# Four edits around TensorE's gaps: a shorter way into the first weights, earlier turned tiles for two output projections, and wider feed-forward matmuls

## The chip, the cores and the metric

One core of one Trainium2 chip runs the whole network for one sequence. The time is that of one execution on the device, in microseconds; kernels are compared by the median of their runs.

The engines each have a queue of their own and meet only at semaphores: TensorE (PE) multiplies and transposes, PEld is its weight load, VectorE (DVE), ScalarE (ACT) and GpSimd (POOL) compute, SyncE (SP) starts most loads.

## The reference

256 tokens, 1024 channels, float32, four layers in a row.

```
x = x + [forgetting attention (16 heads) * silu(ga), dilated attention (16 heads) * silu(gb)] @ even_w_out
x = x + (group_norm(retention(q, k, v), 4 heads of 512) * silu(g)) @ odd_w_out
x = rms_norm(x) ; h = x + rms_norm([ssm mixer, window attention] @ w_out)
h = h + rms_norm((silu(hn @ w_gate) * (hn @ w_up)) @ w_down),  hn = rms_norm(h), D_FF = 2816
```

Before each layer's input projection stands an RMS norm with a gain per channel. `h` is the output. Retention decays with distance, and its result is normalised per token and head before the gate. A row factor of an RMS norm (one number per token) can be applied after a product, since it scales whole rows.

## The kernel before, in words

**Weights.** They are read once, in 232 units of 128 x 1024 numbers (512 KB). A table (`weight_chunks`) puts them in order, in chunks of 4 to 11 units: ga, gb, qa, ka, va, qb, kb, vb (two each), even_out, then rq, rk (two each), rv, rg (four each), odd_out, then the mixer's, then eleven ffn chunks, then down. Four buffers (`RING`) each hold the raw unit (`stage`), its high part (`w_hi`, in the format fp32r, made by ScalarE, line 585) and its low part (`w_lo`, raw less high, by VectorE, line 841). SyncE loads unit u once the low part of unit u - 4 is made. ScalarE splits unit u once TensorE has used unit u - 3. `ahead(name)` on either engine splits up to three units beyond a chunk. An engine's queue is in order, so where a split stands among the other work is part of the design.

**Products.** Activations too have a high and a low part (`act_t`: tiles 0 to 7 high, 8 to 15 low; `y_lo` for the low parts of 16-tile inputs). Every product is made in three passes, high x high, activations' high x weights' low, activations' low x weights' high. `tokens_unit` (line 1404) keeps activations stationary and streams 512 weight columns. `channels_unit` (1421) and `ffn_unit` (1436) keep weights stationary and stream the 256 tokens.

**Turning.** Activations must have channels on partitions. TensorE transposes 128 x 128 blocks against an identity into a PSUM bank, ScalarE copies them as high tiles, VectorE subtracts to get the low ones. `turn_x` with `turn_rows` (1350) does this for x; `turn_wide` (1375) for the 16-tile inputs of even_out and odd_out, all 32 transposes before the first matmul, with `hi_of_wide` (632) and `lo_of_wide` (883) behind.

**Beginning.** TensorE multiplies ones (`keep_busy`, 1458), waits for the identity and the 84 rows of gains and parameters, turns these (1464), multiplies ones again, then turns x. ScalarE splits unit 0, makes eight high tiles, splits unit 1; VectorE likewise with the low ones. POOL issues small loads, `wf` (forget gate weights, 16 columns of a wide matrix) third.

**Heads of the even layer.** `attend` runs the heads through scores, exponentials, transposes and values; each eight heads are gated into gate_a and gate_b by POOL (446) and VectorE (`gate_heads`, 1032; semaphore `heads_out`).

**Retention.** During chunks rv the four heads' scores and values are made, and VectorE centres them (`ret_center`). During chunks rg 0 to 3 ScalarE drains silu(g) into gate1 (724), and VectorE multiplies the normalised head in (`ret_gate`, 1130; `ret_out`): head 0 in chunk rg 1, and so on, head 3 after rg 3.

**Feed-forward.** A chunk is 256 gate and 256 value channels, four units. VectorE takes both from PSUM times the norm's factor of each token (`rstd_row`; 1319), ScalarE applies silu (815), POOL multiplies (562), ScalarE and VectorE split the product (810, 1307) for the down projection. Two chunks' results fit in four banks. `row_of_diag` (1358) makes the factor row after chunk 0.

## Time and profile before

| | us |
|---|---|
| median of 3 runs | 820.35 |
| lowest, highest | 814.86, 823.98 |
| the profiled execution | 818.44 |
| its span | 816.6 |
| TensorE busy | 784.9 (96%) |
| weight load of TensorE, busy | 700.4 (86%) |
| VectorE busy | 520.3 (64%) |
| ScalarE busy | 393.0 (48%) |
| GpSimd busy | 216.8 (27%) |

The busy time of matmuls overlaps, since they are pipelined: the time per matmul is read from the distance of their starts, or from a long piece of the chain divided by its count. An L number is a line of the kernel. The loads move 160 GB/s on average over the span.

### The profile page before, as it was taken

The page shows a single profiled execution, that of the slowest core. Times are in us where ns is not written, and L with a number is a line of the kernel's source. Part 1 is how long each engine was busy: PE and PEld are TensorE (multiplying, and loading weights), DVE is VectorE, ACT ScalarE, POOL GpSimd, SP SyncE. Part 2 cuts the span into 40 slices and gives each one's busy share as a digit, 9 for nine tenths or more (in the row PEclk, how much of TensorE's full clock was granted, in tenths as well). Part 3 has the DMA queues.
Part 4 walks back from the last instruction along what each step waited for, and adds up shares of the span by engine and source line. Part 5 has one row for each costly group of instructions (what it writes and reads, how often), then busy time and mean ns, then how long its engine had stood idle before and what let it go on. Part 6 is the DMA issues. An engine that isn't in the chain of part 4 may idle for free.

```text
span 816.6 us, 13338 instructions
## 1 busy us (share of the span) xinstructions
PE 784.9 (96%) x5469; PEld 700.4 (86%) x5469; DVE 520.3 (64%) x756; ACT 393.0 (48%) x617; POOL 216.8 (27%) x180
## 2 busy tenths in 40 slices
PE   7999999999998999999999899998998999999997
PEld 6789987899877889987778788887777999999885
DVE  4846785864567557866568845775668666666553
ACT  5654446434455454344334535716766443544451
POOL 3022893470811000036019800144002110111010
PEclk9999999999999999999999999999999999999999
DMA  7897892587611554654545455520263665555651
GB/s 212 195 252 208 218 233 75 123 193 170 156 49 54 181 179 155 208 169 143 155 128 180 155 181 181 179 81 2 92 219 124 190 202 181 181 176 185 205 182 51
DMA packets 77824, 130.75 MB, mean 160 GB/s; under 512 B 4415, under 2 KB 28211, under 8 KB 77635
## 3 DMA queue, kind: packets, MB, share of 16 engines
q1 hardware_dynamic: 76418, 125.00, 52.8%
q0 software_dynamic: 1200, 4.83, 2.1%
q8 instruction: 43, 0.70, 0.3%
q14 instruction: 19, 0.15, 0.1%
q10 hardware_dynamic: 144, 0.07, 0.0%
HBM read 128.82 MB, written 1.06 MB: 159 GB/s over the span
## 4 chain that ended last, share of the span: by engine, by line
PE 88%; DVE 7%; DMA 2%; issue 1%; ACT 1%; POOL 1%; SPq 0%; DVEq 0%; POOLq 0%; ACTq 0%
PE ps L1404 41%; PE ps L1421 17%; PE ps L1436 16%; PE ps L1500 2%; PE ps L1519 2%; DMA stage<-in_even_w_in 2%; PE ps L1530 1%; PE ps L1800 1%; PE ps L1532 1%; PE ps L1531 1%; PE ps L1680 1%; DVE w_lo L841 1%; DVE act_t L878 1%; PE ps L1768 1%; PE ps L1630 1%
## 5 line engine op out<-in xcount | busy, mean ns | idle before, releaser
L841 DVE TENSOR_TENSOR w_lo<-stage,w_hi 128x1024 fp32r<-128x1024 f32 x232 | 306.6, 1339 | 177.4 <-ACT w_hi L585 176.9
L585 ACT ACTIVATE w_hi<-stage 128x1024 fp32r<-128x1024 f32 x232 | 244.0, 1062 | 264.6 <-PE ps L1404 129.1
L1404 PE MATMUL ps<-w_hi,act_t 128*128 128x512 f32 (+1 forms) x752 | 246.3, 391 | 3.4 <-DVE act_t L878 2.3
L1404 PEld LDWEIGHTS ps<-w_hi,act_t 128*128 128x128 f32 x752 | 140.6, 188 | 34.6 <-issue 3.6
L1404 PE MATMUL ps<-w_lo,act_t 128*128 128x512 f32 (+1 forms) x440 | 170.1, 387 | 0.0
L1421 PE MATMUL ps<-act_t,w_hi 128*128 128x256 f32 x832 | 151.9, 283 | 0.0
L1421 PEld LDWEIGHTS ps<-act_t,w_hi 128*128 128x128 f32 x832 | 130.8, 193 | 0.2 <-DVE w_lo L841 0.2
L1436 PE MATMUL ps<-act_t,w_hi 128*128 128x256 f32 x704 | 127.2, 283 | 0.7 <-DVE act_t L878 0.7
L1421 PE MATMUL ps<-act_t,w_lo 128*128 128x256 f32 x416 | 117.6, 283 | 0.0
L1436 PEld LDWEIGHTS ps<-act_t,w_hi 128*128 128x128 f32 x704 | 109.9, 192 | 0.9 <-issue 0.9
L1436 PE MATMUL ps<-act_t,w_lo 128*128 128x256 f32 x352 | 99.6, 283 | 0.0
L1404 PEld LDWEIGHTS ps<-w_lo,act_t 128*128 128x128 f32 x440 | 83.1, 189 | 16.8 <-issue 1.0
L1421 PEld LDWEIGHTS ps<-act_t,w_lo 128*128 128x128 f32 x416 | 80.2, 193 | 0.1
L1436 PEld LDWEIGHTS ps<-act_t,w_lo 128*128 128x128 f32 x352 | 67.6, 192 | 0.0
L1404 PE MATMUL ps<-w_hi,y_lo 128*128 128x512 f32 x128 | 50.3, 393 | 0.0
L562 POOL TENSOR_TENSOR big<-big 128x512 f32<-128x512 f32 x11 | 14.3, 1298 | 109.0 <-ACT big L815 109.0
L675 ACT ACTIVATE prob<-prob,neg_max 128x256 f32<-128x256 f32 x40 | 20.2, 505 | 22.5 <-DVE neg_max L1015 22.1
L1404 PE MATMUL ps<-w_hi,ff_hi 128*128 128x512 f32 x76 | 29.6, 389 | 0.0
L1404 PE MATMUL ps<-w_lo,ff_hi 128*128 128x512 f32 x76 | 29.6, 389 | 0.0
L1404 PE MATMUL ps<-w_hi,ff_lo 128*128 128x512 f32 x76 | 29.6, 389 | 0.0
L1404 PEld LDWEIGHTS ps<-w_hi,y_lo 128*128 128x128 f32 x128 | 24.3, 190 | 5.2
L405 POOL TENSOR_TENSOR sumsq<-sumsq,sumsq_b 128x2 f32<-128x2 f32 x2 | 0.4, 196 | 97.6 <-ACT junk L601 97.6
(347 smaller groups left out, 1029.9 us busy)
## 6 DMA issues: line engine op xcount, KB each, us to landing
stage<-in_even_w_in SPq DMA_DIRECT2D x64, 512.0 KB, 5.4
stage<-in_odd_w_in SPq DMA_DIRECT2D x48, 512.0 KB, 4.2
stage<-in_w_gate_up SPq DMA_DIRECT2D x44, 512.0 KB, 4.6
stage<-in_w_down SPq DMA_DIRECT2D x22, 512.0 KB, 4.4
stage<-in_even_w_out SPq DMA_DIRECT2D x16, 512.0 KB, 4.3
stage<-in_odd_w_out SPq DMA_DIRECT2D x16, 512.0 KB, 3.7
stage<-in_w_in SPq DMA_DIRECT2D x10, 512.0 KB, 3.7
stage<-in_w_out SPq DMA_DIRECT2D x8, 512.0 KB, 4.5
```

The source lines that it names most:

```text
L562: nc.gpsimd.tensor_tensor(ff_val[:, c % 2, :], ff_raw[:, c % 2, 0, :], ff_raw[:, c % 2, 1, :], ALU.mult).then_inc(ff_ready, 1)
L585: nc.scalar.activation(w_hi[:, u % RING, :], stage[:, u % RING, :], ACT.Copy).then_inc(hi_ready, 1)
L675: nc.scalar.activation(e[:, 0:256], e[:, 0:256], ACT.Exp, bias=neg_max[:, 1, n:n + 1], scale=-1.0, accum_out=den[:, 1, n:n + 1])
L841: nc.vector.tensor_tensor(w_lo[:, u % RING, :], stage[:, u % RING, :], w_hi[:, u % RING, :].bitcast(F32), ALU.subtract).then_inc(lo_ready, 1)
L878: STT(act_t[:, lo_at + k, :], src, col[:, gain + k:gain + k + 1], act_t[:, at + k, :].bitcast(F32), ALU.mult, ALU.subtract).then_inc(act_l ...
L1404: ins = mm(out[:, b, :], left, right, start=(k == 0 and n == 0), stop=(k == k_tiles - 1 and n == 2))
L1421: ins = mm(o, left, right, start=(k == 0 and n == 0 and m % 2 == 0), stop=(k == k_tiles - 1 and n == 2), skip_group_check=True)
L1436: ins = mm(o, left, right, start=(k == 0 and n == 0 and m == 0), stop=(k == KD - 1 and n == 2), skip_group_check=True)
L1500: even = mm(bank(0, width, at), qs[0][:, tok], ks[0][:, 0:width], start=True, stop=True)
L1519: ins = nc.tensor.transpose(bank(2 + n % 2, P, part * P), prob[:, n % 3, part * P:(part + 1) * P], ident[:])
L1530: mm(bank(out + 1, HD, col_at), e[:, 0:P], v_of(i - 1, 0), start=True, stop=False)
L1531: mm(bank(out + 1, HD, col_at), e[:, P:2 * P], v_of(i - 1, 1), start=False, stop=True)
```

## The change

- **Beginning.** The ones behind the rows are gone, and eleven ones matmuls stand before them in place of four. ScalarE makes two high tiles, splits unit 0, makes two, splits unit 1, makes four, splits unit 2; VectorE follows with the low ones. The `wf` load is issued by POOL behind the landing of unit 1, with a semaphore of its own.
- **Even output projection.** Four of eight double tiles are turned, then matmuls begin; tiles 4 and 5 are turned before unit 1, tiles 6 and 7 before unit 2. VectorE makes the first low tile before the last `gate_heads`. Each of ScalarE and VectorE splits one weight unit in the middle.
- **Retention.** Head h is turned after the third unit of chunk rg h + 1, the last after the second unit of odd_out. The high tiles go to `ret_hi`, which lies on v1, since act_t still holds the input of rg. Banks 4 to 7 are used twice.
- **Feed-forward.** Weights' high half is multiplied with high and low activations in one matmul of 512 columns, weights' low half with the high ones in one of 256. Each chunk has four banks, two chunks all eight. ScalarE copies the part with the low activations out, VectorE adds the other. The norm's factor is multiplied on the gate only; the value's is put on the down projection's output. The factor row is made after unit 2 of chunk 0, and chunk 1 waits for its copy.

```diff
-WARM_BEFORE, WARM_AFTER = 4, 8
+WARM_BEFORE = 11
...
+        ret_hi = over("ret_hi", 4096, [P, 2, RET_H, 2, S], F32R)
...
+        def ffn_result(c, g):
+            at = (4 * (c % 2) + 2 * g) * BANK
+            return ps[:, at:at + 2 * BANK].rearrange("p (m v n) -> p m v n", m=2, v=2)
...
@@ GpSimd @@
+            pool.wait_ge(landed[1], 16)
+            pool.dma_start(wf[...], w_even[...]).then_inc(wf_in, 16)
...
@@ ScalarE, beginning @@
+            hi_of_turned(0, 2, 0, COL_EVEN)
             split_hi(1)
-            hi_of_turned(0, KD, 0, COL_EVEN)
+            hi_of_turned(2, 2, 2, COL_EVEN + 2)
             split_hi(2)
+            hi_of_turned(4, 4, 4, COL_EVEN + 4)
+            split_hi(3)
...
@@ ScalarE, retention (in the loop over chunks rg) @@
+                if c >= 1:
+                    hi_of_ret(c - 1)
+            split_hi(chunks[("odd_out", 0)][0] + 4)
+            hi_of_ret(RET_H - 1)
...
@@ ScalarE, feed-forward @@
                 ahead(("ffn", c))
+                for g in range(2):
+                    act.wait_ge(unit_used, last_unit[("ffn", c)] + g)
+                    nc.scalar.activation(ff_raw[:, c % 2, g, :]..., ffn_result(c, g)[:, :, 1, :], ACT.Copy).then_inc(ff_part, 1)
                 act.wait_ge(ff_raw_ready, c + 1)
...
@@ VectorE, beginning @@
+            lo_of_turned(0, 2, 0, COL_EVEN, KD)
             split_lo(1)
-            lo_of_turned(0, KD, 0, COL_EVEN, KD)
+            lo_of_turned(2, 2, 2, COL_EVEN + 2, KD + 2)
+            split_lo(2)
+            lo_of_turned(4, 4, 4, COL_EVEN + 4, KD + 4)
             split_lo(4)
...
@@ VectorE, even heads, and then before the output projection @@
                     if i % 8 == 3 and i >= 11:
+                        if n == 35:
+                            lo_of_wide(range(1))
                         gate_heads((n - 11) // 8)
...
-            lo_of_wide(KD, EVEN_TURN_BANKS)
+            lo_of_wide(range(1, 4))
+            split_lo(chunks[("even_out", 0)][0] + 4)
+            lo_of_wide(range(4, 8))
...
@@ VectorE, chunks rv and rg @@
                 if step >= 5:
                     ret_gate(step - 5)
+                if step >= 6:
+                    lo_of_ret(step - 6)
...
@@ VectorE, feed-forward @@
-                chunk_done(dve, ("ffn", c))
-                for g in range(2):
-                    ins = TT(ff_raw[:, c % 2, g, :]..., result(("ffn", c))[:, g, :]..., rstd_row[:]..., ALU.mult)
+                dve.wait_ge(ff_part, 2 * c + 1)
+                then(TT(gate, ffn_result(c, 0)[:, :, 0, :], gate, ALU.add))
+                TT(gate, gate, rstd_row[:]..., ALU.mult).then_inc(ff_raw_ready, 1)
+                dve.wait_ge(ff_part, 2 * c + 2)
+                TT(value, ffn_result(c, 1)[:, :, 0, :], value, ALU.add).then_inc(drain_sem(("ffn", c)), 1)
...
@@ TensorE @@
+            def turn_ret(h):
+                pe.wait_ge(ret_out, h + 1)
+                if h >= 2:
+                    pe.wait_ge(act_lo, 2 * KD + 8 + 2 * (h - 1))
+                for i in range(2 * h, 2 * h + 2):
+                    for kk in range(2):
+                        for b in range(NB):
+                            o = ODD_TURN_BANKS[i] * BANK + kk * S + b * P
+                            k = 2 * i + kk
+                            ins = nc.tensor.transpose(ps[:, o:o + P], gate1[:, b, k * P:(k + 1) * P], ident[:])
+                    ins.then_inc(turned, 1)
...
-                        passes = ((hi[:, i, w], act_t[:, k, :]), (lo[:, i, w], act_t[:, k, :]), (hi[:, i, w], act_t[:, KD + k, :]))
+                        mm(o, hi[:, i, w], both[:, :, k, :], start=(k == 0), stop=(k == KD - 1), skip_group_check=True)
+                        ins = mm(o[:, 0, :], lo[:, i, w], act_t[:, k, :], start=False, stop=(k == KD - 1), skip_group_check=True)
...
-            keep_busy(WARM_AFTER)
             pe.wait_ge(x_in, 16 * NB)
...
-            turn_wide(lambda b, k: gate0[...], KD, heads_out, EVEN_TURN_BANKS, even_bank_free)
-            wide_out("even_out", KD)
+            turn_wide(range(4))
+            wide_out("even_out", KD, x_hi, lambda c, j: turn_wide(range(2 * j + 2, 2 * j + 4)) if c == 0 and j in (1, 2) else None)
...
+                    if step >= 5 and j == 2:
+                        if step == 5:
+                            pe.wait_ge(ret_centered, RET_H)
+                        turn_ret(step - 5)
...
-            turn_wide(lambda b, k: gate1[...], 2 * KD + 8, ret_out, ODD_TURN_BANKS, odd_bank_free)
-            wide_out("odd_out", 2 * KD + 8)
+            wide_out("odd_out", 2 * KD + 8, lambda k: ret_hi[...], lambda c, j: turn_ret(RET_H - 1) if (c, j) == (0, 2) else None)
...
             for c in range(11):
                 start_chunk(("ffn", c))
+                if c == 0:
+                    chunk_drained(pe, ("mix_ssm", 1))
+                if c == 1:
+                    pe.wait_ge(row_taken, 4)
```

## Rows read from the trace of the kernel before

**Rows 1.** Page, part 1: busy us, share of the span, instructions

```profile
PE 784.9 (96%) x5469; PEld 700.4 (86%) x5469; DVE 520.3 (64%) x756; ACT 393.0 (48%) x617; POOL 216.8 (27%) x180
```

**Rows 2.** Chain of waits, in order of time: start us, us, what

```profile
301.13 0.87 PE ps L1350 x8
...
635.67 115.19 PE ps L1436 x960
750.86 51.71 PE ps L1404 x228
```

**Rows 3.** Timeline, TensorE, beginning: start us, us, instruction [idle before <-releaser]

```profile
6.40 0.37 PE L1464 MATMUL ps<-ident,rows 84*128 84x84 f32 x1 [3.11 <-DMA rows<-in_vectors]
6.57 3.69 PE L1458 MATMUL ps<-ones 128*128 128x128 f32 x16
...
12.66 0.47 PE L1404 MATMUL ps<-w_hi,act_t 128*128 128x512 f32 x1
...
16.46 0.50 PE L1404 MATMUL ps<-w_hi,act_t 128*128 128x512 f32 x1 [0.81 <-DVE w_lo L841]
...
25.96 0.50 PE L1404 MATMUL ps<-w_hi,act_t 128*128 128x512 f32 x1 [0.29 <-DVE w_lo L841]
```

**Rows 4.** Tile views, first 14 us: x's two loads, then wf's

```profile
DMA to landing us min/median/max: 3.9/4.4/4.8
...
DMA to landing us min/median/max: 5.9/5.9/5.9
```

**Rows 5.** Timeline, ScalarE and VectorE, beginning

```profile
10.81 1.23 DVE L841 TENSOR_TENSOR w_lo<-stage,w_hi 128x1024 fp32r<-128x1024 f32 x1 [3.55 <-ACT w_hi L585]
...
15.18 1.23 DVE L841 TENSOR_TENSOR w_lo<-stage,w_hi 128x1024 fp32r<-128x1024 f32 x1
...
21.76 1.06 ACT L585 ACTIVATE w_hi<-stage 128x1024 fp32r<-128x1024 f32 x1 [1.69 <-DMA stage<-in_even_w_in]
...
24.69 1.22 DVE L841 TENSOR_TENSOR w_lo<-stage,w_hi 128x1024 fp32r<-128x1024 f32 x1
```

**Rows 6.** Timeline, end of the gate chunks and start of odd_out

```profile
459.82 2.78 PE L1375 MATMUL ps<-ident,gate 128*128 128x128 f32 x24
...
461.32 2.77 DVE L1130 SCALAR_TENSOR_TENSOR gate<-v,ret_rstd,gate 128x512 f32<-128x512 f32 x2 [1.51 <-ACT gate L724]
...
464.83 1.55 PE L1375 MATMUL ps<-ident,gate 128*128 128x128 f32 x8 [2.23 <-DVE y_lo L883]
466.04 0.78 PE L1404 MATMUL ps<-w_hi,act_t 128*128 128x512 f32 x1
...
469.10 0.40 PE L1404 MATMUL ps<-w_lo,act_t 128*128 128x512 f32 x1
```

**Rows 7.** Timeline, start of even_out

```profile
258.86 2.06 ACT L632 ACTIVATE act_t<-ps 128x512 fp32r<-128x512 f32 x4 [4.02 <-PE ps L1375]
...
259.69 1.23 DVE L1032 TENSOR_TENSOR gate_b<-ps,gate_b 128x1024 f32<-128x1024 f32 x1 [2.09 <-POOL gate_b L446]
...
261.06 1.94 PE L1375 MATMUL ps<-ident,gate_b 128*128 128x128 f32 x16 [0.93 <-DVE gate_b L1032]
```

**Rows 8.** Timeline, VectorE, in chunk rg 2

```profile
442.05 1.76 DVE L1130 SCALAR_TENSOR_TENSOR gate<-v,ret_rstd,gate 128x512 f32<-128x512 f32 x2
443.73 6.10 DVE L841 TENSOR_TENSOR w_lo<-stage,w_hi 128x1024 fp32r<-128x1024 f32 x3
```

**Rows 9.** Timeline, VectorE and ScalarE, ffn chunk 0 and then chunk 3

```profile
630.34 0.48 DVE L860 TENSOR_SCALAR diag<-ident,rstd 128x128 f32<-128x128 f32 x2 [0.87 <-POOL rstd L407]
...
633.53 1.23 DVE L841 TENSOR_TENSOR w_lo<-stage,w_hi 128x1024 fp32r<-128x1024 f32 x1 [0.44 <-ACT w_hi L585]
...
670.26 1.29 DVE L1319 TENSOR_TENSOR big<-ps,rstd_row 128x512 f32<-128x512 f32 x2 [0.50 <-PE ps L1436]
...
671.52 0.62 ACT L810 ACTIVATE ff_hi<-big 128x512 fp32r<-128x512 f32 x1
672.05 2.22 ACT L585 ACTIVATE w_hi<-stage 128x1024 fp32r<-128x1024 f32 x2
```

More of the change, by code:

```diff
@@ L626, in out_and_turn, with hi_of_ret, hi_of_wide @@
                 hi_of_turned(first + 4, 4, 4, gain + 4)
-            def hi_of_wide(first, banks):
-                for i in range(8):
-                    act.wait_ge(turned, first + i + 1)
-                    nc.scalar.activation(act_t[:, 2 * i:2 * i + 2, :], bank(banks[i]).rearrange("p (k n) -> p k n", k=2), ACT.Copy).then_inc(act_hi, 1)
+            def hi_of_ret(h):
+                for b in range(2):
+                    act.wait_ge(turned, 2 * KD + 8 + 2 * h + b + 1)
+                    nc.scalar.activation(ret_hi[:, b, h, :, :], bank(ODD_TURN_BANKS[2 * h + b]).rearrange("p (k n) -> p k n", k=2), ACT.Copy).then_inc(act_hi, 1)
+            def hi_of_wide(parts):
+                for i in parts:
+                    act.wait_ge(turned, KD + i + 1)
+                    nc.scalar.activation(act_t[:, 2 * i:2 * i + 2, :], bank(EVEN_TURN_BANKS[i]).rearrange("p (k n) -> p k n", k=2), ACT.Copy).then_inc(act_hi, 1)
             act.dma_start(ident[:], t["ident"]).then_inc(ident_in, 16)
@@ L703, in _ @@
                         ahead((v, 1))
-            hi_of_wide(KD, EVEN_TURN_BANKS)
+            hi_of_wide(range(4))
+            split_hi(chunks[("even_out", 0)][0] + 4)
+            hi_of_wide(range(4, 8))
             out_and_turn("even_out", 1, KD + 8, COL_ODD)
@@ L878, in lo_of_turned, with lo_of_wide, lo_of_ret @@
                     STT(act_t[:, lo_at + k, :], src, col[:, gain + k:gain + k + 1], act_t[:, at + k, :].bitcast(F32), ALU.mult, ALU.subtract).then_inc(act_lo, 1)
[L880 to L883 removed]
+            def lo_of_wide(parts):
+                for i in parts:
+                    dve.wait_ge(act_hi, KD + i + 1)
+                    TT(y_lo[:, 2 * i:2 * i + 2, :], bank(EVEN_TURN_BANKS[i]).rearrange("p (k n) -> p k n", k=2), act_t[:, 2 * i:2 * i + 2, :].bitcast(F32),
+                       ALU.subtract).then_inc(act_lo, 1)
+            def lo_of_ret(h):
+                for b in range(2):
+                    dve.wait_ge(act_hi, 2 * KD + 8 + 2 * h + b + 1)
+                    TT(y_lo[:, 4 * h + 2 * b:4 * h + 2 * b + 2, :], bank(ODD_TURN_BANKS[2 * h + b]).rearrange("p (k n) -> p k n", k=2),
+                       ret_hi[:, b, h, :, :].bitcast(F32), ALU.subtract).then_inc(act_lo, 1)
             nc.vector.memset(half_pi[:], PI / 2)
@@ L1144, in _ @@
             ret_gate(RET_H - 1)
-            lo_of_wide(2 * KD + 8, ODD_TURN_BANKS)
+            lo_of_ret(RET_H - 2)
+            split_lo(chunks[("odd_out", 0)][0] + 4)
+            lo_of_ret(RET_H - 1)
             out_and_turn("odd_out", 2 * KD + 16, COL_MIX)
@@ L1426, in ffn_unit @@
                 hi, lo = unit_of(name, j)
+                both = act_t[:, :, :].rearrange("p (v k) n -> p v k n", v=2)
                 for i in range(4):
@@ L1582, in wide_out @@
                     for j in range(8):
+                        late(c, j)
                         if (c, j) == (1, 6):
```

82 lines of the change are left out of this document (34 added, 48 removed).

## The prediction

> **What bounds the kernel now.** I read the page's busy shares first. TensorE is busy for 96% of the span [rows 1], so only two things shorten this kernel: less matmul time, or fewer of TensorE's gaps, 816.6 - 784.9 = 31.7 us in all. Then the chain of waits, whose long pieces give prices at full clock [rows 2]: a 512-column matmul 51.71/228 = 0.227 us, a 256-column one 115.19/960 = 0.120, a group of eight transposes 0.87, so 0.109 each. A unit of 12 wide matmuls is 2.72 us. Then the timeline at each place that the diff touches.
>
> **Beginning.** TensorE idles 3.11 us for the rows, transposes them at 6.40, does 16 instructions for eight ones matmuls (3.5 us until about 10.05, 0.22 each), turns x, and starts real matmuls at 12.66 [rows 3]. x was issued at 0.7 and 1.2 us and landed 3.9 to 4.8 us later [rows 4], by 6.0: its transposes stood behind the ones, not behind the load. They move to about 6.8. Eleven ones matmuls ahead of the rows are 22 x 0.22 = 4.9 us from 1.2, over at 6.1, before the rows land: no cost.
>
> That alone gains little, for the low half of weight unit 0 is ready at 10.81 + 1.23 = 12.04 [rows 5] in both kernels. The turned tiles, which came after it, now come before it: first matmul 12.05. The reordering matters more one unit later. The low half of unit 1 stood at 15.18, behind eight low tiles, and TensorE waited 0.81 us for it [rows 3, 5]; now it stands behind two (0.4 each) and ends near 12.04 + 0.8 + 1.23 = 14.1, not 16.41. That frees a stage buffer 2.3 us sooner, so unit 5 comes 2.3 us before 21.76. ScalarE is held by unit 5 ahead of the small exponential that VectorE needs, and VectorE's split of unit 4 (24.69 to 25.91) is queued behind that; for it TensorE waits at 25.96 [rows 3, 5]. It moves to 23.6. TensorE itself needs 12.05 + 4 x 2.72 + 0.65 (the row matmuls) = 23.6. So up to 2.3 us.
>
> Against it stands the clock. The 16 ones instructions took 0.22 each, twice the 0.109 of a 128-column one later: the clock was 1.2 GHz, and rose while x was turned, after work without a break since 6.40. Now TensorE works from 1.2 to 6.1, turns x until 8.5 (10.3 at half clock), and has nothing until 12.05. At the odd layer 24 transposes and 2.23 us of idling were followed by half clock [rows 6]. I expect the same here: some 3 us of real matmuls at half speed, 1.4 lost. **I take 0.9 us of gain** (2.3 - 1.4); ends: 0 (the gain eaten by cold units) and 2.3.
>
> The Trainium skill ("TensorE: Matmul & The Clock Gate", "Part 1: The HAM clock gate" and "Part 4: PE-mode transpose") says that idling puts TensorE back to half clock, and that transposes don't count as work for it. By that rule the beginning is cold for certain; the half clock of rows 6 agrees, though it can't separate the two reasons.
>
> The wf load leaves the front of POOL's queue for behind the landing of unit 1. Its 64 KB took 5.9 us to land [rows 4]; even issued at 14 it is there by 20, and ScalarE asks for it after 22, behind the same exponential and the sines. VectorE's wait for parameters no longer includes it. POOL, waiting for unit 1, delays only the norm's root, whose squares end near 17. No cost; that units 0 and 1 might land sooner is left to the range.
>
> **Even output projection.** All 32 transposes come first: 16 until 261.06 - 0.93 = 260.1, an idle 0.93 us for the last gated heads, 16 more, matmuls from 261.06 + 1.75 = 262.8 [rows 7]. After the change unit 0 needs one low tile, which stands ahead of the last gating on VectorE: high copy at 258.86 for 0.5, low 0.6, done at 260.0. The gating, which waits for POOL until 259.69 anyway, slips 0.3 to 261.2, and the second low tile is there at 261.8. Unit 0 runs 260.1 to 262.8; then transposes 4 and 5 wait for nothing. No transpose is saved, only the idle: **0.9 us** (0 to 1.0). Late next would be unit 3, low half by 264.5, wanted at 270.
>
> **Retention.** From the last gate chunk to the first output matmul it is 459.82 to 466.04, 6.22 us, of which 32 x 0.109 = 3.5 are transposes: 2.7 go to waiting and half clock. The seven matmuls up to 469.10 took 3.06 us where 7 x 0.227 = 1.6 was due, 1.5 more [rows 6]. With three heads turned inside chunks rg 1 to 3 and the fourth after two output units, matmuls follow at once: the last gating ends at 464.1 [rows 6], the turn is at 460.7 + 5.4 = 466.1. Transposes are paid in either place. **4.2 us**; ends: 1.2 (rival C) and 4.3.
>
> What is queued behind the added work? Chunk rg 2 runs on TensorE from 459.82 - 2 x 10.9 = 438.0. ScalarE gates (2 x 0.63, to 439.5), makes two new high copies (1.1) and the split (1.06): 441.7. VectorE: split 2.0 at most, gate 1.76 [rows 8]: 445.5, where TensorE asks for the gated head at 438.0 + 3 x 2.72 = 446.2. Then two low tiles 1.3 and a split 6.10/3 = 2.0: 448.8, wanted at 449.8. So 0.7 and 1.0 us are spare. Stage buffers come free 1 to 2 us later; the load still lands before its split is due. The ret_hi tile lies on v1, each part written after the gate has read it: no new wait.
>
> **Feed-forward.** Three 256-column matmuls (0.360) become one of 512 and one of 256 (0.347): 0.013 x 352 = **4.6 us**. The 512 columns are now two runs of 256, eight tiles apart, which no row shows. Ends: it costs as two (no gain), or 0.227. I take the nearest row, of the same width and bank. The Trainium skill (same page, "Back-to-back issue gap") gives N/2.4 + 2.5 ns for a matmul by itself; by it merging would save 2.5 ns a time, 0.9 us in all. The trace's 13 ns over N/2.4 at both widths disagrees.
>
> Added per chunk: two copies on ScalarE (0.6 each) and one operation on VectorE (0.65), in a chain that ScalarE's next split stands behind: copy 0.6, add 0.65, multiply 0.65, silu 0.63, high 0.62, split 1.11, then the low split 1.23 [rows 9]: 5.5 us from the chunk's end if nothing overlaps, against 3 units x 2.77 = 8.3 that TensorE has in hand. Hidden, 2.8 to spare. The row matmuls of chunk 0 come a unit earlier: diag is ready at 630.8, TensorE is there at 632.3. Chunk 1 then waits for the row's copy: VectorE's split ends at 634.8 [rows 9], the copy at 635.2, chunk 0 at 635.3. Nothing. In the tail a multiply becomes a fused one, 0.06 longer, beside POOL's root: nothing.
>
> **Sum.** 0.9 + 0.9 + 4.2 + 4.6 = 10.6 us; later stages follow TensorE's progress, so gains add. The profiled run took 818.44 us (span 816.6), 1.9 below the median 820.35; single runs lie between 814.86 and 823.98. I start from between the two, 819.4: **808.8 us**.
>
> **Rivals.** (B) The wide matmul costs as much as two, or merging saves only the 0.9: 812.5 to 813.4. For: no row with split columns. Against: the same overhead at both widths. (C) VectorE is late in the gate chunks. One gate took 2.77 us against 1.76 [rows 6, 8], and splits run from 1.2 to 2.0 with POOL beside them: 1 us for each of three chunks, and nothing from the beginning: 812.7. (D) The clock holds at the beginning: 1.4 more, 807.4. Against: the idling. (E) Slower: in the feed-forward the drain, now through ScalarE, VectorE and ScalarE again, outlasts the three units in hand. It decides from 8.3 us on; at 10.0 every chunk loses 1.7, eleven 19 us: 827.5, and 832 without the 4.6. Against: 5.5 us by rows.
>
> **Chances.** Forecast 0.45, B 0.19, C 0.21, D 0.10, E 0.05. Within 1% is 812.1 to 828.6, about what this measurement can tell from no change. A median may lie 2.5 us off, which leaves 0.38 of the forecast, 0.09 of D and 0.13 of B and C for faster: faster 0.60, slower 0.04, same 0.36. Range: 807.4 less 2.5 and a sooner landing, 804, to 813.4 plus 2.5, 816.
>
> **What would show it.** The changed profile should have: x turned from about 6.8 us, matmuls from 12.05 with 0.43 us steps at first, unit 4 begun between 23.6 and 25; no idle before the even transposes; 0.87 us groups of transposes inside rg 1 to 3 and no half clock behind them; 0.347 us per pair in the feed-forward, about 122 us for 127. The forecast is wrong if the pair takes 0.36, if TensorE waits for gated heads or low halves in rg 1 to 3, or if idle time grows elsewhere.

## The result and the profile after

| | us | runs |
|---|---|---|
| kernel before, median (lowest, highest) | 821.48 (814.86, 824.53) | 21 |
| changed kernel, median (lowest, highest) | 814.02 (808.66, 820.71) | 21 |
| ratio after / before, 95% interval | 0.9925 [0.9902, 0.9947] | |
| profiled execution of the changed kernel, its span | 815.45, 813.6 | 1 |

The change gains 0.75%, some 6 us. I forecast 808.8 us, 10.6 us or 1.3% below my starting point of 819.4, and 1.5% below the median measured here: the right direction and little over half of the size. The two profiled spans lie 3.0 us apart, less than the medians, and the reason is the granted clock of the two executions, 0.992 over the span before and 0.987 after, which is worth 4 us.

The page of the changed kernel, part 1 (busy us, share, instructions), beside [rows 1]:

```profile
PE 783.8 (96%) x5115; PEld 683.6 (84%) x5115; DVE 525.3 (65%) x767; ACT 403.6 (50%) x640; POOL 218.1 (27%) x180
```

TensorE has 354 matmuls fewer (352 of the feed-forward, and two of the ones), yet is busy only 1.1 us less. VectorE and ScalarE took on 5.0 and 10.6 us; my prices per chunk, times eleven, had said 7 and 13.

Timeline of TensorE at the beginning of the changed kernel (columns as in [rows 3], which it answers):

```profile
1.22 5.06 PE L1515 MATMUL ps<-ones 128*128 128x128 f32 x22 [1.22 <-DVE neg_half L927]
6.60 0.37 PE L1521 MATMUL ps<-ident,rows 84*128 84x84 f32 x1 [0.32 <-DMA rows<-in_vectors]
6.77 1.98 PE L1396 MATMUL ps<-ident,x 128*128 128x128 f32 x16
11.11 0.47 PE L1462 MATMUL ps<-w_hi,act_t 128*128 128x512 f32 x1 [2.37 <-DVE w_lo L871]
...
22.10 0.60 PE L1404 MATMUL ps<-diag,ones 128*128 128x128 f32 x4
26.25 0.50 PE L1462 MATMUL ps<-w_hi,act_t 128*128 128x512 f32 x1 [3.55 <-DVE w_lo L871]
```

Up to 22.1 us it goes better than I said: matmuls start at 11.11 instead of 12.66, and four units and the row are done at 22.7. Then TensorE waits 3.55 us for the low half of unit 4, which comes 0.3 us *later* than before. ScalarE and VectorE there ([rows 5]), in the timeline:

```profile
22.06 1.06 ACT L596 ACTIVATE w_hi<-stage 128x1024 fp32r<-128x1024 f32 x1 [3.33 <-DMA stage<-in_even_w_in]
23.02 0.20 ACT L666 ACTIVATE sp_dt<-sp_ldt 128x16 f32<-128x16 f32 x1
...
23.25 0.18 DVE L953 TENSOR_TENSOR sp_mdt<-sp_lre,sp_dt 128x16 f32<-128x16 f32 x1 [2.81 <-ACT sp_dt L666]
...
24.98 2.35 DVE L871 TENSOR_TENSOR w_lo<-stage,w_hi 128x1024 fp32r<-128x1024 f32 x2
```

The tile views of SP's load of unit 5, and of wf:

```profile
L381 SPq DMA_DIRECT2D stage<-in_even_w_in x1: 368/368/368, 13.6 to 13.6; - x1
...
DMA to landing us min/median/max: 8.4/8.4/8.4
...
L409 POOL DMA_DIRECT2D wf<-in_even_w_in x1: 921/921/921, 11.6 to 11.6; - x1
...
DMA to landing us min/median/max: 7.8/7.8/7.8
```

Read upwards from the wait: the low half of unit 4 stands on VectorE behind a chain of small operations, these wait for ScalarE's exponential, and ScalarE waits for unit 5. Unit 5 was issued at 13.64, 2.8 us sooner than the 16.43 of before, as I said it would be, and landed at 22.0: 8.4 us where the load of before took 5.3. What lies beside it is wf, issued at 11.6 and 7.8 us under way. Unit 4, issued at 11.0, ahead of wf, took 5.3.

The even output projection (timeline) and the turned retention heads (chain of waits: start us, us, what), for [rows 7] and [rows 6]:

```profile
259.93 1.92 PE L1420 MATMUL ps<-ident,gate_a 128*128 128x128 f32 x16
262.04 0.47 PE L1462 MATMUL ps<-w_hi,act_t 128*128 128x512 f32 x1 [0.20 <-DVE y_lo L914]
```

```profile
436.57 0.87 PE ps L1433 x8
437.45 10.91 PE ps L1462 x48
...
460.15 0.87 PE ps L1433 x8
461.02 8.18 PE ps L1462 x36
469.20 0.87 PE ps L1433 x8
470.08 32.69 PE ps L1462 x144
502.77 0.87 PE ps L1396 x8
```

Here each line is what I forecast: groups of 0.87 us, units of 10.91/4 = 2.73 us directly behind them, no idle before them, and 227 ns a matmul (32.69/144), so no half clock. The next turned x stands at 302.20 behind the even projection (301.13 in [rows 2], +1.07) and at 502.77 behind the odd one (505.79 before, -3.02). The retention part gained 4.09 us; I had taken 4.2.

The granted clock by stretches (window, its us, busy us of TensorE (matmuls), granted clock, DMA share, GB/s), first the changed kernel, then the kernel before:

```profile
24.00:34.00 10.00, 7.75 (x27) 0.83 0.65 184
147.00:160.00 13.00, 11.57 (x88) 0.87 0.45 122
...
440.00:480.00 40.00, 40.00 (x190) 1.00 0.55 180
545.00:560.00 15.00, 11.44 (x63) 0.77 0.01 2
615.00:630.00 15.00, 12.47 (x58) 0.77 0.28 86
```

```profile
24.00:34.00 10.00, 9.71 (x45) 1.00 0.86 217
147.00:160.00 13.00, 11.24 (x97) 1.00 0.64 151
...
440.00:480.00 40.00, 37.77 (x176) 0.96 0.50 161
545.00:560.00 15.00, 11.88 (x78) 0.89 0.10 35
615.00:630.00 15.00, 11.80 (x82) 1.00 0.24 74
```

A mean of 0.77 over 15 us is 2 x 0.23 x 15 = 6.9 us at 1.2 GHz. The retention stage lost its half clock (0.96 to 1.00, 3.2 us of it); no profile with the new retention part has any there, and of the three with the old part two have it (before and ffn_only) and one, begin_only, hasn't. The changed kernel has new half clock behind the 3.55 us idle (24 to 34), and more in the mixer (545 to 560), a stage that the change doesn't touch, and from 615 to 630. The stretch from 147 to 160 (0.87) lies in the heads of the even layer, untouched too: nine of the twelve profiles with the new beginning have half clock there, and none of the three with the old one, which this document doesn't explain.

That last stretch isn't the feed-forward's doing either. The clock falls while x is turned ahead of it, behind waits for VectorE of 1.50 and 0.30 us which the kernel before has too (at 616.67 and 617.63 here, at 619.15 and 620.11 there), where the clock held. Eleven of the fifteen profiles that can be read show half clock in this place, out_only's and ffn_only's among them. Before, begin_only, exp_first and after_third don't.

**A measure that takes the clock out.** Single runs of one kernel spread over 10 us, and their clock goes with it: the kernel before has runs of 814.4 us at a mean clock of 0.998 and of 822.8 at 0.985. So beside each median I give, as means over the runs, the half-clock time, 2 x (1 - clock) x time, and the *full-clock time*, time x clock, which is the time less half of the half-clock time (exact only where TensorE was busy in it). Its standard error is 0.2 us for the kernel before and 0.35 to 0.7 for the others. Left out are runs over 850 us, and three runs over 1.5% above the fastest of their kernel (two of begin_only, with which its median is 827.39, and one of exp_first).

| kernel | runs | median | ratio to before | half-clock time | full-clock time |
|---|---|---|---|---|---|
| before, the four times it ran beside the others | 21 to 29 | 818.3 to 820.7 | | 13.9 to 18.2 | 811.2 to 811.7 |
| changed | 21 | 814.02 | 0.9925 | 18.5 | 804.4 |
| changed, once more (after_third) | 12 | 813.42 | 0.9921 | 18.6 | 804.1 |
| begin_only | 10 | 825.71 | 1.0095 | 25.4 | 812.4 |
| begin_mended | 11 | 816.24 | 0.9985 | 18.4 | 808.0 |
| out_only | 12 | 815.36 | 0.9967 | 16.8 | 807.4 |
| ffn_only | 12 | 817.77 | 0.9959 | 20.1 | 807.25 |
| wide_contig | 12 | 814.16 | 0.9927 | 20.0 | 804.6 |
| wf_front | 6 | 811.53 | 0.9893 | 20.3 | 801.8 |
| exp_first | 5 | 809.85 | 0.9866 | 12.7 | 803.5 |
| both_early | 12 | 810.96 | 0.9915 | 21.7 | 800.4 |
| hhll | 8 | 809.78 | 0.9897 | 19.5 | 800.2 |
| gap_busy | 11 | 809.15 | 0.9899 | 15.5 | 802.3 |
| all_three | 9 | 810.54 | 0.9900 | 18.6 | 801.9 |

The 21 runs of the kernel before in the first table have no clock on record. The full-clock gain of the changed kernel is therefore taken against the 811.6 of the kernel before in other runs: 7.2 us. For after_third, which has the kernel before beside it (811.65), it is 7.5.

### The profile page after: what moved, and what is told of

It reads as the page before. It is cut to its first block, busy times and chain, and to the rows that moved or that the text cites. A ratio compares the mean times of both kernels' runs of the same rounds, so it can differ in the third digit from the quotient of the medians.

```text
span 813.6 us, 12652 instructions
## 1 busy us (share of the span) xinstructions
PE 783.8 (96%) x5115; PEld 683.6 (84%) x5115; DVE 525.3 (65%) x767; ACT 403.6 (50%) x640; POOL 218.1 (27%) x180
## 4 chain that ended last, share of the span: by engine, by line
PE 89%; DVE 5%; DMA 2%; issue 2%; ACT 1%; POOL 0%; SPq 0%; DVEq 0%; POOLq 0%; ACTq 0%
PE ps L1462 41%; PE ps L1479 17%; PE ps L1492 10%; PE ps L1493 5%; DMA stage<-in_even_w_in 2%; PE ps L1556 2%; PE ps L1575 2%; PE ps L1586 1%; PE ps L1588 1%; PE ps L1587 1%; PE ps L1855 1%; PE ps L1739 1%; DVE w_lo L871 1%; PE ps L1819 1%; PE ps L1683 1%
## 5 line engine op out<-in xcount | busy, mean ns | idle before, releaser
L871 DVE TENSOR_TENSOR w_lo<-stage,w_hi 128x1024 fp32r<-128x1024 f32 x232 | 303.3, 1325 | 168.6 <-ACT w_hi L596 168.1
L1462 PE MATMUL ps<-w_hi,act_t 128*128 128x512 f32 (+1 forms) x688 | 221.9, 392 | 8.4 <-DVE w_lo L871 5.9
L1462 PEld LDWEIGHTS ps<-w_hi,act_t 128*128 128x128 f32 x688 | 129.0, 189 | 36.2 <-issue 6.6
L1479 PE MATMUL ps<-act_t,w_hi 128*128 128x256 f32 x832 | 151.9, 284 | 0.0
L1462 PE MATMUL ps<-w_lo,act_t 128*128 128x512 f32 (+1 forms) x376 | 145.3, 387 | 0.0
L1479 PEld LDWEIGHTS ps<-act_t,w_hi 128*128 128x128 f32 x832 | 130.8, 193 | 0.3 <-DVE w_lo L871 0.2
L1492 PE MATMUL ps<-act_t,w_hi 128*128 128x512 f32 x352 | 126.0, 402 | 0.3 <-DVE act_t L908 0.3
L1462 PEld LDWEIGHTS ps<-w_lo,act_t 128*128 128x128 f32 x376 | 71.1, 189 | 14.5 <-issue 1.0
L1492 PEld LDWEIGHTS ps<-act_t,w_hi 128*128 128x128 f32 x352 | 66.9, 190 | 17.3 <-issue 0.6
L908 DVE SCALAR_TENSOR_TENSOR act_t<-ps,col,act_t 128x256 fp32r<-128x256 f32 x40 | 16.7, 477 | 14.7 <-ACT act_t L623 14.7
```

What stands on the lines that cost most here:

```text
L871: nc.vector.tensor_tensor(w_lo[:, u % RING, :], stage[:, u % RING, :], w_hi[:, u % RING, :].bitcast(F32), ALU.subtract).then_inc(lo_ready, 1)
L908: STT(act_t[:, lo_at + k, :], src, col[:, gain + k:gain + k + 1], act_t[:, at + k, :].bitcast(F32), ALU.mult, ALU.subtract).then_inc(act_l ...
L1462: ins = mm(out[:, b, :], left, right, start=(k == 0 and n == 0), stop=(k == k_tiles - 1 and n == 2))
L1479: ins = mm(o, left, right, start=(k == 0 and n == 0 and m % 2 == 0), stop=(k == k_tiles - 1 and n == 2), skip_group_check=True)
L1492: mm(o, hi[:, i, w], both[:, :, k, :], start=(k == 0), stop=(k == KD - 1), skip_group_check=True)
```

## The experiments

**The load of wf (wf_front).** The changed kernel, with one load back at its old place:

```diff
             pool.dma_start(parity ...
+            pool.dma_start(wf[...], w_even[... fa ...]).then_inc(wf_in, 16)
             pool.dma_start(bf[:], ...).then_inc(params_in, 16)
...
-            pool.wait_ge(landed[1], 16)
-            pool.dma_start(wf[...], w_even[... fa ...]).then_inc(wf_in, 16)
```

> The changed kernel with the wf load (64 KB in 64-byte pieces) issued third on GpSimd's queue, as before the change, and not behind unit 1. Theory A: in the changed kernel this load, issued at 11.6 us, shares the queues with the loads of units 4 and 5, and unit 5 took 8.4 us to land where 5.3 were needed before; ScalarE, VectorE and TensorE wait behind it. Then here unit 5 lands in about 5.3 us, TensorE's 3.55 us wait ahead of unit 4 shrinks under 2 us, matmuls of unit 4 begin near 24 and not at 26.2, and the half clock at 27 to 31 us is gone: 2 to 4 us less than the changed kernel, about 0.988 of the kernel before. Theory B (the loads are simply slow there, all queues being full): unit 5 takes 8 us here too, unit 0 lands 0.9 us later (9.6, not 8.7), unit 4 begins at 26 or later: same as the changed kernel, 0.9925, or 1 us more.

Measured: 811.53 us, ratio 0.9893 [0.9862, 0.9924]; 2.6 us less full-clock time than the changed kernel. In its trace unit 5 landed 6.4 us after its issue at 13.4, TensorE's wait was 1.6 us instead of 3.55, unit 4 began at 24.0, and no half clock followed (1.00 over 24 to 34). That is theory A, with one share of B: unit 5 still took 1.1 us more than the 5.3 of the kernel before.

One trace is little, so here is the same load in every profile with the new beginning, with what I read from the tile views: from the issue of wf, of unit 4 and of unit 5 to their landing (the issue in brackets), all in us.

| kernel | wf | unit 4 | unit 5 | TensorE's wait before unit 4 |
|---|---|---|---|---|
| changed | 7.8 (11.6) | 5.3 (11.0) | 8.4 (13.6) | 3.55 |
| after_third | 8.0 (11.5) | 5.0 (11.1) | 8.6 (13.6) | 3.70 |
| after_again | 7.0 (11.8) | 5.0 (11.1) | 7.6 (13.9) | 1.41 |
| exp_first | 9.2 (11.0) | 5.2 (11.0) | 10.3 (13.1) | none |
| exp_again | 8.2 (11.7) | 10.7 (12.3) | 12.0 (14.2) | 1.64 |
| begin_only | 9.7 (11.2) | 11.5 (11.7) | 12.8 (13.7) | 7.24 |
| wide_contig | 4.8 (12.8) | 5.0 (11.2) | 5.6 (14.9) | 0.18 |
| five with wf early | 6.4 to 7.1 (2.5) | 4.9 to 5.1 | 6.0 to 6.5 (13.2 to 13.8) | 0.28 to 1.64 |

With wf in front of it unit 5 took 7.6 to 12.8 us in six profiles of seven, and unit 4 took 10.7 and 11.5 where it too was issued behind wf (begin_only, exp_again). In the seventh, wide_contig, wf was quick (4.8 us) and unit 5 hardly slower than before. So the load of wf is a cause, and how much it costs differs from run to run; why it was quick once isn't shown.

**ScalarE's order (exp_first).** The changed kernel, the exponentials ahead of what waits for unit 5:

```diff
-            split_hi(6)
+            split_hi(5)
             act.wait_ge(ldt_ready, 1)
             nc.scalar.activation(sp["dt"][:], sp["ldt"][:], ACT.Exp).then_inc(dt_ready, 1)
             act.wait_ge(mdt_ready, 1)
             nc.scalar.activation(sp["mag"][:], sp["mdt"][:], ACT.Exp).then_inc(mag_ready, 1)
+            split_hi(6)
```

> The changed kernel, with ScalarE's two small exponentials put ahead of its split of unit 5, nothing else. If TensorE waits at 22.7 to 26.2 us because VectorE's split of unit 4 is queued behind a chain that waits for unit 5's landing (theory A), the split of unit 4 comes at about 22 us, the wait of 3.55 us becomes under 1 us, the half clock behind it goes too, and the kernel is 3 to 5 us faster than the changed one (about 0.987 of the kernel before), whatever unit 5's load takes, unless TensorE then waits for unit 5 itself (lands at 22.1, its low half at 24.6 or so, wanted at 25.4). Theory B (TensorE is bound by the rate of the loads, and the order of the queues is only where it shows): the wait moves to units 5 to 7 and the sum of TensorE's waits up to 40 us stays near 6 us, the time at 0.9925.

Measured: 809.85 us, ratio 0.9866 [0.9831, 0.9902]; full-clock time 803.5, 0.9 below the changed kernel with a standard error of 0.75, so most of that ratio is the clock in five runs. The trace shows theory A's mechanism: unit 5 was even slower here (10.3 us), yet VectorE's split of unit 4 came at 21.5 us and TensorE didn't wait for it. The next wait for a low half, 1.30 us, stands at 33.7.

**Both mends (both_early).**

> The changed kernel with both mends of its beginning: wf loaded third on POOL's queue again, and ScalarE's two exponentials ahead of its split of unit 5. Theory A (the load of wf, in small pieces, slows that of unit 5, and ScalarE's order passes this on to VectorE and so to unit 4): unit 5 lands some 6 us after it is issued, unit 4 is begun by 23.9 us, TensorE waits for neither, 810.5 us, little below either mend alone (811.5 and 810.6), since each alone removes most of one idle stretch of 3.5 us. Theory B (the two mends each gained by luck of the clock or of the pair time): the same 814 as the changed kernel.

Measured: 810.96 us, ratio 0.9915 [0.9884, 0.9946]. The full-clock time, 800.4, is 4.0 below that of the changed kernel, about the sum of the two mends (2.6 + 0.9), and the median is near theory A's 810.5. By the ratio alone theory B isn't excluded: the kernel before ran at 818.27 beside this one, and 0.9915 lies within the interval of the changed kernel. Timeline of TensorE:

```profile
10.87 0.47 PE L1462 MATMUL ps<-w_hi,act_t 128*128 128x512 f32 x1 [2.44 <-DVE w_lo L871]
...
23.46 0.50 PE L1462 MATMUL ps<-w_hi,act_t 128*128 128x512 f32 x1 [0.75 <-DVE w_lo L871]
```

The tile view of the load of unit 5, issued at 13.8:

```profile
DMA to landing us min/median/max: 6.0/6.0/6.0
```

Unit 4 begins at 23.46, 2.5 us before the 25.96 of [rows 3]. That is what my term for the beginning had described.

**Each part alone.** The kernel before with the beginning alone, unmended (begin_only), with both output projections alone (out_only), and with the feed-forward alone (ffn_only). Their edits are the parts of the change's own diff; for begin_only:

```diff
-WARM_BEFORE, WARM_AFTER = 4, 8
+WARM_BEFORE = 11
...
+            hi_of_turned(0, 2, 0, COL_EVEN)
             split_hi(1)
-            hi_of_turned(0, KD, 0, COL_EVEN)
+            hi_of_turned(2, 2, 2, COL_EVEN + 2)
             split_hi(2)
+            hi_of_turned(4, 4, 4, COL_EVEN + 4)
+            split_hi(3)
```

and the same for the low halves, and wf behind the landing of unit 1.

> The kernel before with the beginning of the change alone (no ones behind the rows, copies and splits in the new order, wf behind the landing of unit 1). My term said 0.9 us of gain. By the trace of the changed kernel it is a loss: unit 4 begun 0.3 us later, then half clock for 3.4 us from 27.3, 1.7 us later at the end of the first stage. So theory A: 0 to 2 us slower than the kernel before (1.000 to 1.0024). Rival (clock by chance): 0.9 to 2 us faster, 0.9989 to 0.9976.

Measured: 825.71 us, ratio 1.0095 [1.0056, 1.0134]: a loss of some 8 us, four times what theory A allowed. Only 0.7 us of it is full-clock time; 11.5 us more half-clock time give another 5.7. (In its trace about 2.7 us of the half clock, 28 to 30.67 us, fell into idling, so some of the lost waiting is booked there as clock.) Its trace, from an execution of 821.01 us (timeline of TensorE and ScalarE):

```profile
22.82 0.60 PE L1365 MATMUL ps<-diag,ones 128*128 128x128 f32 x4
30.67 0.79 PE L1411 MATMUL ps<-w_hi,act_t 128*128 128x512 f32 x1 [7.24 <-DVE w_lo L845]
...
23.25 1.06 ACT L586 ACTIVATE w_hi<-stage 128x1024 fp32r<-128x1024 f32 x1 [5.68 <-DMA stage<-in_even_w_in]
26.47 1.06 ACT L586 ACTIVATE w_hi<-stage 128x1024 fp32r<-128x1024 f32 x1 [2.17 <-DMA stage<-in_even_w_in]
```

The tile view of its load of unit 5:

```profile
L371 SPq DMA_DIRECT2D stage<-in_even_w_in x1: 368/368/368, 13.7 to 13.7; - x1
DMA to landing us min/median/max: 12.8/12.8/12.8
```

The same load, issued at the same 13.7 us, took 12.8 us here, 8.4 in the changed kernel and 6.0 with wf early, and unit 4, issued 0.5 us behind wf, took 11.5; TensorE idled 7.24 us. This execution had a clock of 0.992, 13 us of half-clock time, where the mean of the ten runs is 25.4: where the other runs lost theirs I can't show, as this one alone was traced.

> The kernel before with both output projections of the change (the even one begun with the first turned tiles, the retention heads turned inside the gate chunks), its beginning and its feed-forward as before. By my terms 0.9 + 4.2 = 5.1 us less than the kernel before: ratio 0.9938. By the changed kernel's trace 4.1 for retention alone. Rival (lost later): the transposes inside the gate chunks keep the clock up there, but half clock comes instead in a later stage, and the time is within 2 us of the kernel before (0.9976 or more).

Measured: 815.36 us, ratio 0.9967 [0.9932, 1.0003], full-clock time 807.4, 4.3 us below the kernel before. My 5.1 held 1.6 us of half clock in the retention stage, which this measure doesn't count, so 3.5 is what it has to be held against. In plain time the gain isn't clear of noise: the interval ends at 1.0003, and half-clock time was 16.8 us against 13.9 beside it. Its trace has none in the retention stage and some at 545 to 555 and 615 to 625, as the rival said, so the rival isn't excluded for the clock's share. Both steps can be read in the changed kernel above.

> The kernel before with the feed-forward part of the change alone (wide matmuls, eight banks, new drain). From the changed trace a pair takes 0.3535 us, not 0.347: theory A is that this is all, so the feed-forward takes 2.3 us less (chunks of 11.31 us, not 11.52) and the kernel is at 0.997 of the one before. Theory B: another part of the change costs it elsewhere (half clock at its start by the earlier order of the mixer, the row of chunk 0): then 0.999 to 1.001.

Measured: 817.77 us, ratio 0.9959 [0.9926, 0.9992], full-clock time 807.25, 4.2 us less than before (forecast 4.6). The 2.3 us of theory A were too few, and its chunks took 11.10 us in the trace, not 11.31; why comes below. The full-clock parts add up within their errors: +0.7 - 4.3 - 4.2 = -7.8 for a changed kernel that measured -7.2 and -7.5.

**The beginning alone, mended (begin_mended):** begin_only with the two edits of both_early.

> The kernel before with the beginning of the change alone, wf third on POOL's queue as before and the exponentials ahead of ScalarE's split of unit 5. Theory A (the load of wf, and the order that passes its lateness on, are the whole loss): unit 4 is begun at about 24 us instead of 25.96, the product of time and mean granted clock is 1 to 3 us below that of the kernel before (811.6), ratio 0.996 to 0.999, 8 to 10 us less than the unmended beginning (827.4). Theory C (without the ones behind the rows the clock itself is in a worse state later): half-clock time stays near the 27 us of begin_only against 14 to 18 of the kernel before, ratio 1.003 or more.

Measured: 816.24 us, ratio 0.9985 [0.9956, 1.0014]; full-clock time 808.0, 3.7 us below the kernel before and 4.4 below begin_only; the ratio is 0.011 lower, 9 us. Half-clock time 18.4 us, back from 25.4, against 15.5 for the kernel before beside it. So wf's place and ScalarE's order were the loss at full clock and most of the loss through the clock; the last 3 us of half-clock time (1.5 us) may belong to the missing ones or to chance. There is no trace of it that can be read (the profiled execution took 2934 us), so where unit 4 began in it isn't shown.

**Why a pair takes two different times.** In the changed kernel a chunk of the feed-forward took 11.31 us, 32 pairs of 0.3534, not 0.347. VectorE's multiply, once a chunk, and TensorE in the changed kernel, then the same rows of exp_first:

```profile
668.81 0.69 DVE L1367 TENSOR_TENSOR big<-big,rstd_row 128x512 f32<-128x512 f32 x1
680.11 0.69 DVE L1367 TENSOR_TENSOR big<-big,rstd_row 128x512 f32<-128x512 f32 x1
...
671.84 0.28 PE L1493 MATMUL ps<-act_t,w_lo 128*128 128x256 f32 x1
671.96 0.40 PE L1492 MATMUL ps<-act_t,w_hi 128*128 128x512 f32 x1
672.20 0.28 PE L1493 MATMUL ps<-act_t,w_lo 128*128 128x256 f32 x1
672.31 0.40 PE L1492 MATMUL ps<-act_t,w_hi 128*128 128x512 f32 x1
```

```profile
666.19 0.69 DVE L1368 TENSOR_TENSOR big<-big,rstd_row 128x512 f32<-128x512 f32 x1
677.29 0.69 DVE L1368 TENSOR_TENSOR big<-big,rstd_row 128x512 f32<-128x512 f32 x1
...
671.88 0.28 PE L1494 MATMUL ps<-act_t,w_lo 128*128 128x256 f32 x1
671.99 0.39 PE L1493 MATMUL ps<-act_t,w_hi 128*128 128x512 f32 x1
672.22 0.28 PE L1494 MATMUL ps<-act_t,w_lo 128*128 128x256 f32 x1
```

At full clock in both, the starts step by 230 and 117 ns in exp_first (11.10 us a chunk), and in a cycle of three pairs in the changed kernel. I first suspected the two separate runs of 256 columns, and put high and low tiles side by side (wide_contig; the copies that write the tiles are changed alike):

```diff
-                both = act_t[:, :, :].rearrange("p (v k) n -> p v k n", v=2)
+                both = act_t[:, :, :].rearrange("p (k v) n -> p k v n", v=2)
...
-                        mm(o, hi[:, i, w], both[:, :, k, :], ...)
+                        mm(o, hi[:, i, w], both[:, k, :, :], ...)
```

> The changed kernel with the feed-forward's high and low activation tiles stored next to each other, so that the 512 columns of the wide matmul are one run. Theory A (reading two runs of 256, eight tiles apart, costs 7 ns a matmul): a pair takes 0.347 us, a chunk 11.1 and not 11.31, 2.3 us less in all, 0.9897 of the kernel before. Theory B (it is the alternation of a 512 and a 256 column matmul with their weight loads, or both operands' ports): a pair stays at 0.353 and the time at 0.9925.

Measured: 814.16 us, ratio 0.9927 [0.9899, 0.9955], a chunk in 11.30 us: the layout is not it, my theory fell. Then the same kernels once more, unedited:

> The changed kernel once more, nothing edited. The question: a pair of the feed-forward (512 and 256 columns) took 0.3534 us in the profiled run of the changed kernel and in two of its variants, and 0.3467 us in two others, at the same granted clock. If it is a state of the single run (theory R), a second profile of the same kernel may show either; a chunk period of 11.10 us (0.3467) would prove it. If it belongs to the program, its layout or the place of its instructions (theory K), the chunk period is 11.31 us again (0.3534).

> The variant with the exponentials first once more, nothing edited. Its first profile had the rhythm of 0.3467 us a pair. Theory P (the rhythm belongs to the program): 0.3467 again, 230 and 117 ns. Theory S (it is a state of the single run, entered at the start of the feed-forward): either may show, and 0.3534 would prove it.

Measured: after_again 0.3534 again (one execution, 823.51 us at a clock of 0.972: 46 us of half-clock time), exp_again 0.3534, where exp_first, the same program, had 0.3467. The third profile of the changed kernel settles it from the other side: 0.3467 in after_third.

> The changed kernel, nothing edited, beside the kernel before and the mended beginning. If the parts add (beginning -0.9 to -1.1 worse in time times clock, output projections 4.3 better, feed-forward 4.4 better), the product of time and mean granted clock is 7 to 7.7 us below that of the kernel before, and the ratio is 0.990 to 0.994. The feed-forward may show either rhythm.

Measured: 813.42 us, ratio 0.9921 [0.9889, 0.9953]. Unit 5 took 8.6 us and TensorE idled 3.70 us before unit 4, as in the first profile. So the pair time is a state of the single run, worth 352 x 6.7 ns = 2.4 us, and not of the program. Of ten profiles with the alternating order seven show the slow one (changed, after_again, exp_again, wide_contig, wf_front, both_early, gap_busy) and three the fast one (after_third, exp_first, ffn_only). Last, like widths issued together (hhll, on both_early):

```diff
                     for m in range(2):
                         o, w = ...
                         mm(o, hi[:, i, w], both[:, :, k, :], ...)
+                    for m in range(2):
+                        o, w = ...
                         ins = mm(o[:, 0, :], lo[:, i, w], act_t[:, k, :], ...)
```

> The changed kernel with both mends of its beginning (wf third on POOL's queue, exponentials ahead of ScalarE's split of unit 5), and in the feed-forward the two 512-column matmuls of a k tile issued together, ahead of the two 256-column ones, where they alternated. In the trace the alternating pairs run in one of two rhythms at full clock: 230 and 117 ns (0.3467 a pair), or a cycle of three pairs of 236, 114, 232, 118, 240, 120 ns (0.3534 a pair). Theory R (the rhythm comes from the alternation of the two widths): with like widths together the steps are those that each width has elsewhere, 227 and 120 ns, 0.347 a pair, a chunk in 11.10 us. Theory K (the two runs of 256 columns in the moving tile cost it): 0.3534 again. If R holds and both_early ran at 0.3534 in most of its runs, 2.3 us less than both_early (810.96 with before at 818.27, ratio 0.9915), so about 0.989; if K, 0.9915.

VectorE's multiply, chunk by chunk, in hhll:

```profile
653.21 0.69 DVE L1367 TENSOR_TENSOR big<-big,rstd_row 128x512 f32<-128x512 f32 x1
664.35 0.69 DVE L1367 TENSOR_TENSOR big<-big,rstd_row 128x512 f32<-128x512 f32 x1
```

Measured: 11.15 us a chunk (0.3483 a pair), the same in all_three; ratio 0.9897 [0.9863, 0.9932], full-clock time 800.2 against 800.4 for both_early. The order sets another rhythm near the fast one, but a gain in time isn't shown. Why the alternating order falls into one or the other stays open.

**Ones in the gap (gap_busy, all_three).** On both_early: `keep_busy(8, 3)` behind `turn_x(4)`, eight ones matmuls into bank 3 while TensorE waits for unit 0; all_three adds hhll's order.

> The changed kernel with both mends of its beginning, and eight ones matmuls (1.8 us at full clock) behind the turned x, in bank 3, in the 2.4 us in which TensorE waits for the low half of unit 0. Their product is not used. Theory C (the idle stretches at the beginning give the clock its occasion to fall: three profiles of nine with the new beginning show half clock from 11 to 15.6 us): no half clock before 30 us, half-clock time over the runs less than both_early's mean of 22 us, ratio 0.989 to 0.991. Rival (the clock falls no later for work of this kind, or falls elsewhere instead): ratio as both_early, 0.9915, or up to 1 us worse where the ones run at half clock into the first real matmul.

> Both edits on top of the two mends: like widths together in the feed-forward, and eight ones matmuls behind the turned x. If each holds: ratio 0.987 to 0.989 (about 808 to 809.5 us where the kernel before takes 818.3), the best version. If neither: 0.9915.

Measured: 809.15 us, ratio 0.9899 [0.9866, 0.9933], and 810.54, 0.9900 [0.9868, 0.9932]. The granted clock of gap_busy and then of exp_again, both from 10 to 20 us:

```profile
10.00:20.00 10.00, 9.51 (x44) 1.00 1.04 229
```

```profile
10.00:20.00 10.00, 7.63 (x27) 0.83 0.94 200
```

Of ten profiles with the new beginning and the gap, four have half clock starting between 11.4 and 12.3 us (after_again, exp_first, exp_again, wide_contig) and six don't; of the two with ones in the gap, none. That is too few to call it shown, and the profiled run of gap_busy, at a mean clock of 0.982, had 29 us of half-clock time later on. By its numbers gap_busy came out as theory C said (15.5 us of half-clock time against 21.7, ratio 0.9899), but the full-clock time rose by 1.9 us over both_early, and by 1.7 from hhll to all_three, each with a standard error near 0.9; where the ones would cost something isn't shown: in gap_busy's trace the first real matmul (10.90) and unit 4 (23.34) come no later than in both_early's. The versions between 0.9866 and 0.9915 can't be told apart by these runs. All lie below the changed kernel's 0.9925 by their point values, with intervals that overlap its own; that both_early beats it rests on the trace and on 4.0 us of full-clock time.

## Why the prediction was off

**Beginning: forecast 0.9 gained (2.3 at full clock, less 1.4 for half clock), measured 0.7 lost at full clock and more through the clock.** Three of its steps held: x turned from 6.77 us (6.8 said), first matmul at 11.11 (12.05 said; unit 0 landed 0.9 us sooner, at 8.70), unit 5 issued 2.8 us sooner (2.3). The step that failed is "No cost" for the load of wf. I asked only when wf would be there, and it was there in time. I didn't ask what 64 KB that take 5.9 us to land [rows 4] do to the load beside them: unit 5 took 8.4 us instead of 5.3 (5.6 to 12.8 in six other profiles), and all of the head start was gone. ScalarE's order, which I had described as the reason why unit 4 waits for unit 5, passed it on unchanged; I named it as the path of the gain and not as the path of a loss. With both mended the part is worth 3.7 us at full clock, above my upper end of 2.3.

**The clock at the beginning.** I took 1.4 us for half clock from 12.05 on, and gave rival D (the clock holds) 0.10. In the first profile D's mechanism happened: 2.37 us idle behind the transposes, then steps of 0.23 us. In four of ten profiles it went my way. Which of the two a run gets is chance as far as these runs show, and 0.10 for D was too low for six of ten. The Trainium skill ("TensorE: Matmul & The Clock Gate", "Part 4: PE-mode transpose") says that transposes don't count as work for the gate; by that the beginning would be cold every time, and six profiles of ten disagree. What cost more were the 3.55 us of idling at 22.7, with half clock behind them, which no step of mine contained.

**Even projection: the mechanism right, 0.65 of the 0.9 in the trace.** The 0.93 us of idling before the second 16 transposes are gone, 0.20 is left before the first matmul. From the first transposes to the next turned x it takes 42.27 us (259.93 to 302.20) and took 42.92 (258.21 to 301.13). **Retention: 4.2 against 4.09 in the trace.** No wait of TensorE in rg 1 to 3, so rival C's place stayed quiet. VectorE was slow as C had warned: its gates took 2.11, 3.48, 1.76 and 2.47 us, and the second, from 444.60 on, ended 0.3 us before TensorE turned that head at 448.36. That is closer than the 0.7 us that I had counted as spare, so C was missed by little. Both projections together: 4.3 at full clock, 3.5 by my terms without the half clock.

**Feed-forward: 4.6 against 4.2 at full clock**, and 2.3 in the first profile (0.360 - 0.3534, times 352). The nearest row gave the right price for one rhythm; that there are two no row of before could show, because equal widths keep one (11.52 us a chunk in the profiles of before, out_only and begin_only). The 4.2 lies between the 2.3 of the slow rhythm and the 4.7 of the fast one. Rival B, whose time (812.5 to 813.4) is nearest to the 814.02 measured, is wrong by its mechanism: the wide matmul doesn't cost as much as two. Its lower variant, 0.9 us in all from the 2.5 ns a matmul of the Trainium skill ("TensorE: Matmul & The Clock Gate", "Back-to-back issue gap"), is too small by ffn_only's 4.2 us. The longer drain through ScalarE and VectorE cost nothing, as worked out: TensorE has no wait in the steady chunks, so rival E's point was never near.

**The sum.** "Later stages follow TensorE's progress, so gains add" holds at full clock, where the parts measured alone make -7.8 and the whole -7.2 to -7.5. It says nothing of the clock, and that is the second step that failed. My 10.6 us were 10.4 at full clock (2.3 + 0.9 + 2.6 + 4.6) and 0.2 from the clock (1.6 gained in the retention stage, 1.4 lost at the beginning). At full clock the beginning fell 3.0 short, the feed-forward 0.4, and the projections came out 0.8 higher. The clock lost where I had it gain: half-clock time is 18.6 us in after_third against 15.5 in the kernel before beside it, 1.5 us of time, although the retention stage no longer has any. In the two profiled runs the changed kernel had 6.9 us of half-clock time each at 545 to 560 and 615 to 630, where the kernel before had 3.3 and 0. Why the clock falls there more often isn't shown.

## What to carry to other kernels

When a load is moved, ask what it does to the loads that it now runs beside, not only whether it arrives in time; loads that take long for their size are the suspects. An engine's order that passes on a gain passes on a loss as well, so take what nobody needs to wait for out from behind a load. Where runs of one kernel differ by more than the effect, multiply each run's time by its granted clock: parts measured alone then add up, which their medians do not.

## What the runs showed that I had not expected

- The same 512 KB load, issued at 13.1 to 14.9 us, took 6.0 to 6.5 us in five profiles with wf issued at 2.5, and with wf (64 KB) issued some 2 us ahead of it 7.6, 8.4, 8.6, 10.3, 12.0 and 12.8 us in six profiles and 5.6 in a seventh. It was slowest where wf itself was slow (7.0 to 9.7 us) and quick where wf was quick (4.8).
- 512- and 256-column matmuls in alternation run at 0.3467 or 0.3534 us a pair at the same clock, and one unedited program shows either in different executions.
- A change confined to the first 26 us (begin_only) raised the half-clock time of the whole run by 11.5 us, and took 825.7 us where the same work in mended order took 816.2.
- Behind the same transposes and 2.2 to 3.8 us of idling the clock fell to 1.2 GHz in four profiles of ten and held in six. Idles of 2.37 and 2.57 us (changed, after_third) were followed by full clock, and one of 2.40 (exp_first) by half clock.
